# Gate and up products with the weight tiles stationary, and the down product between the two half units

## The reference

```python
D_MODEL = 1024
SEQ = 256
FFN_DIM = 2816            # D_FF = 2816 in the second block

def rmsnorm(x, g):
    xf = x.astype(jnp.float32)
    y = xf * lax.rsqrt(jnp.mean(xf * xf, axis=-1, keepdims=True) + RMS_EPS)
    return (y * g.astype(jnp.float32)).astype(x.dtype)

def swiglu(h, w_gate, w_up, w_down):
    return (jax.nn.silu(h @ w_gate) * (h @ w_up)) @ w_down

# first block
        ff = (jax.nn.silu(h @ w_ffn_gate[i]) * (h @ w_ffn_up[i])) @ w_ffn_down[i]
        x = x + rms_norm(ff, norm_ffn_post[i])
# second block, twice in each layer, with a residual weight of 0.5
        h = h + FFN_RESIDUAL_WEIGHT * swiglu(rmsnorm(h, ffn1_norm[layer]),
                                             ffn1_w_gate[layer], ffn1_w_up[layer], ffn1_w_down[layer])
```

## Time and profile before

| | |
|---|---|
| median of 3 runs | 1906.07 us (1905.44 to 1907.4) |
| span of the profiled execution, first to last instruction | 1904.2 us |
| PE busy | 1868.7 us, 98% of the span, 8988 matmuls |
| DVE busy | 1107.1 us, 58% |
| ACT busy | 958.9 us, 50% |
| POOL busy | 150.4 us, 8% |
| DMA | 332.72 MB, mean 175 GB/s |

### The profile page before, as it was taken

The page is one execution under the profiler, slowest core; times in us unless marked ns, Lnnn a source line. Parts: engine busy times, 40 slices in busy tenths (PEclk is TensorE's granted clock), DMA queues, the critical chain, the costliest instruction groups (busy, mean ns, idle before and its releaser), DMA issues.

```text
span 1904.2 us, 26150 instructions
## 1 busy us (share of the span) xinstructions
PE 1868.7 (98%) x8988; PEld 1523.3 (80%) x8988; DVE 1107.1 (58%) x1365; ACT 958.9 (50%) x1277; POOL 150.4 (8%) x259
## 2 busy tenths in 40 slices
PE   8999999999999999999999999999999999999998
PEld 7777888887877888888788887788888888868887
DVE  6666565448676575446754456655465445575454
ACT  5664454445675464445544446644454444564443
POOL 5210010001300010000100012000011000100000
PEclk9999999999999999999999999999999999999999
DMA  6335565554524546565655554455565564526553
GB/s 225 123 119 184 179 217 190 178 183 151 166 90 166 205 164 204 193 198 177 201 190 178 179 202 141 143 195 179 182 219 170 184 198 169 195 90 197 178 178 107
DMA packets 204987, 332.72 MB, mean 175 GB/s; under 512 B 11360, under 2 KB 150240, under 8 KB 204896
## 3 DMA queue, kind: packets, MB, share of 16 engines
q1 hardware_dynamic: 200240, 319.08, 49.9%
q0 software_dynamic: 3120, 11.02, 1.7%
q10 hardware_dynamic: 1536, 1.47, 0.2%
HBM read 330.48 MB, written 1.05 MB: 174 GB/s over the span
## 4 chain that ended last, share of the span: by engine, by line
PE 88%; issue 4%; DVE 3%; ACT 3%; DMA 1%; POOL 0%; DVEq 0%; SPq 0%; POOLq 0%; ACTq 0%
PE ps L571 27%; PE ps L565 27%; PE ps L556 27%; PE ps L598 3%; ACT whi L1254 1%; PE ps L771 1%; PE ps L759 1%; PE ps L787 1%; ACT prob L1352 1%; DVE wlo L1738 1%; DMA raw<-w_in_dram 0%; DVE prob L1878 0%; DMA xs<-x_dram 0%; DVE prob L1851 0%; DVE act_lo L1744 0%
## 5 line engine op out<-in xcount | busy, mean ns | idle before, releaser
L1738 DVE TENSOR_TENSOR wlo<-raw,whi 128x2048 fp32r<-128x2048 f32 (+1 forms) x306 | 690.6, 2257 | 510.3 <-ACT whi L1254 509.8
L1254 ACT ACTIVATE whi<-raw 128x2048 fp32r<-128x2048 f32 (+1 forms) x306 | 576.9, 1885 | 422.4 <-PE ps L565 422.3
L571 PE MATMUL ps<-whi,act_hi 128*128 128x512 f32 (+2 forms) x1632 | 442.0, 392 | 5.1 <-issue 2.4
L556 PE MATMUL ps<-wlo,act_hi 128*128 128x512 f32 (+2 forms) x1632 | 438.7, 387 | 0.0
L565 PE MATMUL ps<-whi,act_lo 128*128 128x512 f32 (+2 forms) x1632 | 432.2, 386 | 1.5 <-DVE act_lo L1744 1.5
L565 PEld LDWEIGHTS ps<-whi,act_lo 128*128 128x128 f32 x1632 | 303.9, 188 | 64.4 <-DVE act_lo L1744 2.3
L556 PEld LDWEIGHTS ps<-wlo,act_hi 128*128 128x128 f32 x1632 | 302.2, 188 | 61.8 <-issue 1.1
L571 PEld LDWEIGHTS ps<-whi,act_hi 128*128 128x128 f32 x1632 | 297.5, 188 | 64.1 <-issue 2.8
L1299 ACT ACTIVATE hid<-ps,stat 128x256 f32<-128x256 f32 x132 | 62.6, 474 | 282.9 <-PE ps L598 197.4
L2320 POOL TENSOR_TENSOR stat<-stat,eps 128x1 f32<-128x1 f32 x43 | 22.4, 521 | 1471.4 <-ACT prob L1286 1471.1
L1791 DVE SCALAR_TENSOR_TENSOR hid<-ps,stat,hid 128x256 f32<-128x256 f32 x132 | 63.6, 482 | 123.7 <-ACT hid L1299 123.7
(11 more groups left out here) (217 smaller groups left out, 1611.5 us busy)
## 6 DMA issues: line engine op xcount, KB each, us to landing
raw<-ffn_w_gate_dram SPq DMA_DIRECT2D x88, 512.0 KB, 4.0
raw<-ffn_w_up_dram SPq DMA_DIRECT2D x88, 512.0 KB, 5.0
raw<-ffn_w_down_dram SPq DMA_DIRECT2D x88, 512.0 KB, 3.9
raw<-w_in_dram SPq DMA_DIRECT2D x64, 512.0 KB, 4.4
raw<-w_ffn_gate_dram SPq DMA_DIRECT2D x44, 512.0 KB, 4.0
raw<-w_ffn_up_dram SPq DMA_DIRECT2D x44, 512.0 KB, 5.0
raw<-w_ffn_down_dram SPq DMA_DIRECT2D x44, 512.0 KB, 3.9
raw<-a_w_qkv_dram SPq DMA_DIRECT2D x24, 512.0 KB, 4.5
```

The lines of the kernel that those rows point to most:

```text
L556: last = nc.tensor.matmul(o, hi, a, start=False, stop=last_pass and stop and i == len(parts) - 1)
L571: nc.tensor.matmul(o, hi, a, start=start and i == 0, stop=False)
L1254: nc.scalar.activation(whi[:, u % SLOTS, 0:words], raw[:, u % SLOTS, 0:words], ACT.Copy)\
L1738: nc.vector.tensor_tensor(wlo[:, u % SLOTS, 0:words], raw[:, u % SLOTS, 0:words], whi[:, u % SLOTS, 0:words].bitcast(F32), ALU.subtract)\
```

## The change

Chunk 0 of a feed-forward part is computed as before. In chunks 1 to 10 gate and up take a 128x128 tile of weights as the stationary operand and the activations as the moving one (`columns`). The results come out turned, hidden features on the partitions and tokens along the columns, so nothing has to be transposed. `act_hi` and `act_lo` now lie side by side in one tile, and for each weight tile there are two matmuls: the hi weights against hi and lo activations at once (512 columns), and the lo weights against the hi activations (256 columns, added to the first half of the bank). A chunk's gate and up use four banks (0 to 3), and each unit is used in one go. The down product stands between the two units, and SP loads in that order.

The norm's factor is now along the columns. It is brought there once in each feed-forward part: DVE multiplies the identity by the factor (`spread_scale`), PE multiplies a tile of ones by that (`spread_scales`, two 128x128 matmuls), ACT copies the result. ACT copies the lo half of a bank to SBUF (`low_half`), DVE adds the hi half (`sum_parts`), DVE multiplies gate by the factor (`times_scale`), ACT takes silu, DVE multiplies by up, ACT rounds to `hid_hi`, DVE writes `hid_lo`. The up product's factor is left out and applied at the end of the feed-forward part, through the factor `fold` or `scale_of` in instructions that were there already. POOL has one memset more at the start.

```diff
                 gu(u, 0, 0)
                 gu(u + 1, 4, 0)
-                gu(u + 2, 0, CH)
-                gu(u + 3, 4, CH)
-                down(u + 4, 0)
-                with sp.Fori(0, NCH - 3) as i:
+                with sp.Fori(0, NCH - 2) as i:
                     w.chunk = i
-                    gu(u + 5, 0, i * CH + 2 * CH)
-                    gu(u + 6, 4, i * CH + 2 * CH)
-                    down(u + 7, i * CH + CH)
+                    gu(u + 2, 0, i * CH + CH)
+                    down(u + 3, i * CH)
+                    gu(u + 4, 4, i * CH + CH)
...
+                def spread_scales(tn):
+                    for t in range(T):
+                        free_before("turn", tn + t)
+                        pe.wait_ge(sem("spread"), w.at("spread", nth * T + t + 1))
+                        nc.tensor.matmul(ps[:, 2 + (tn + t) % 2, 0:P], ones[:, :], diagonal[:, t, :],
+                                         start=True, stop=True).then_inc(sem("turn_done"), 1)
...
+                def columns(u, half, gu, between=None, by_columns=False):
+                    unit_there(u)
+                    at = (slice(None), u % SLOTS, slice(None))
+                    vh, vl = (b[at].rearrange("p (k g n) -> p k g n", k=4, g=2) for b in (whi, wlo))
+                    order = [(g, j) for g in range(2) for j in range(CH // P)]
+                    if by_columns:
+                        order.sort(key=lambda at: at[1])
+                    for n, (g, j) in enumerate(order):
+                        if half == 0 and between is None and j == 0:
+                            free_before("gu", gu + g)
+                        elif half == 0 and g == 0 and between is not None:
+                            was_read("gu", gu - 2 + j)
+                        elif half == 0 and j == 0 and between is not None:
+                            between()
+                        bank = ps[:, 2 * g + j, :]
+                        cols = slice(j * P, (j + 1) * P)
+                        for k in range(4):
+                            kt = 4 * half + k
+                            nc.tensor.matmul(bank.rearrange("p (a n) -> p a n", a=2), vh[:, k, g, cols], both[:, :, kt, :],
+                                             start=half == 0 and k == 0, stop=False)
+                            last = nc.tensor.matmul(bank[:, 0:S], vl[:, k, g, cols], act_hi[:, kt, :],
+                                                    start=False, stop=half == 1 and k == 3)
+                        if half == 1 and n % 2 == 1:
+                            last.then_inc(sem("gu_done"), 1)
+                    if half == 0:
+                        last.then_inc(sem("used"), 1)
...
-                def chunk(u, gu, tn, start):
-                    tile = gate_up(u, gu)
-                    tile(0)
-                    turn_hidden(gu - T, tn)
-                    tile(1)
-                    down(u + 2, tn, start=start)
+                nth = gu // (2 * NCH)
+                _, diagonal, _ = scale_places(w)
                 tile = gate_up(u, gu, ready)
                 tile(0)
                 tile(1)
-                chunk(u + 2, gu + 2, tn, True)
+                def first_hidden():
+                    turn_hidden(gu, tn)
+                    spread_scales(tn + T)
+                    for t in range(T):
+                        was_read("turn", tn + T + t)
+                columns(u + 2, 0, gu + 2, first_hidden)
+                down(u + 3, 0)
+                columns(u + 4, 1, gu + 2)
                 with pe.Fori(0, NCH - 3) as i:
                     w.chunk = i
-                    chunk(u + 5, gu + 4, tn + 2, False)
+                    columns(u + 5, 0, gu + 4)
+                    down(u + 6, 1)
+                    columns(u + 7, 1, gu + 4)
                 w.chunk = None
-                u, gu, tn = u + UNITS_FFN - 4, gu + 2 * (NCH - 1), tn + 2 * (NCH - 1)
-                turn_hidden(gu - T, tn - T)
-                tile = gate_up(u, gu)
-                tile(0)
-                tile(1, (0,))
-                down(u + 2, tn - T, tiles=(0,))
-                turn_hidden(gu, tn, tiles=(0,))
-                tile(1, (1,))
-                down(u + 3, tn, tiles=(0,), stop=True)
-                turn_hidden(gu, tn, tiles=(1,))
-                down(u + 2, tn - T, tiles=(1,))
+                u, gu = u + UNITS_FFN - 4, gu + 2 * (NCH - 1)
+                columns(u, 0, gu)
+                columns(u + 1, 1, gu, by_columns=True)
+                down(u + 2, NCH - 2, tiles=(0,))
+                down(u + 3, NCH - 1, tiles=(0,), stop=True)
+                down(u + 2, NCH - 2, tiles=(1,))
                 if by_columns:
-                    down_by_columns(u + 3, tn)
+                    down_by_columns(u + 3, NCH - 1)
                 else:
-                    down(u + 3, tn, tiles=(1,), stop=True, between=between)
+                    down(u + 3, NCH - 1, tiles=(1,), stop=True, between=between)
...
+                for t in range(T):
+                    turned_hi(tn + t, hid_hi[:, :, t * P:(t + 1) * P], CH // P)
+                for t in range(T):
+                    turned_copy(tn + T + t, scale_row[:, t * P:(t + 1) * P].unsqueeze(1), 1)
+                with act.Fori(0, NCH - 2) as i:
                     w.chunk = i
-                    chunk(gu + 4, tn + 2)
+                    split(2)
+                    low_half(3, hid, 0)
+                    columns_silu(1)
+                    low_half(4, up_sum, 1)
+                    columns_hi(2)
+                    split(1)
                 w.chunk = None
-                done[0] += 3 * (NCH - 4)
-                last = NCH - 1
-                gu, tn = gu + 2 * last, tn + 2 * last
-                hidden_hi(tn - T)
-                silu(gu, 0, tn - T)
-                split(1)
-                hidden_hi(tn, (0,), tail[:, 0])
-                silu(gu, 1, tn - T)
-                split(1)
-                hidden_hi(tn, (1,), tail[:, 0])
+                done[0] += 3 * (NCH - 3)
+                split(1)
+                act.wait_ge(sem("hidden_lo"), w.at("hidden_lo", nth * NCH + NCH - 2))
+                for j in range(CH // P):
+                    js = slice(j, j + 1)
+                    low_half(2 * NCH - 1 + j, hid, 0, js)
+                    low_half(2 * NCH - 1 + j, up_sum, 1, js)
+                    columns_silu(2 * (NCH - 2) + 2 * j + 1, hid[:, j, :])
+                    columns_hi(2 * (NCH - 2) + 2 * j + 2, hid[:, j, :], tail[:, 0, j, :])
+                split(1)
...
+                def sum_parts(dst, g, js=slice(0, CH // P)):
+                    return nc.vector.tensor_tensor(dst, ps[:, 2 * g:2 * g + 2, 0:S][:, js, :], dst, ALU.add)
...
+                def columns(c):
+                    low_there(2 * c - 1)
+                    sum_parts(hid[:, :, :], 0).then_inc(sem("gu_read_v"), 1)
+                    was_summed(2 * c + 1)
+                    times_scale()
+                    low_there(2 * c)
+                    sum_parts(up_sum, 1).then_inc(sem("gu_read_v"), 1)
+                    was_summed(2 * c + 2)
+                    times_silu(T + c)
+                def hidden_lo(n, src=hid[:, :, :], lo=hid_lo[:, :, :], hi=hid_hi[:, :, :]):
+                    dve.wait_ge(sem("hidden_hi"), w.at("hidden_hi", nth * NCH + n))
+                    rest(lo, src, hi).then_inc(sem("hidden_lo"), 1)
+                def last_columns(c, j):
+                    js = slice(j, j + 1)
+                    low_there(2 * c - 1 + 2 * j)
+                    sum_parts(hid[:, js, :], 0, js).then_inc(sem("last_sum"), 1)
+                    low_there(2 * c + 2 * j)
+                    sum_parts(up_sum[:, js, :], 1, js).then_inc(sem("gu_read_v"), 1)
+                    dve.wait_ge(sem("last_sum"), w.at("last_sum", nth * (CH // P) + j + 1))
+                    times_scale(js)
+                    was_summed(2 * c + 1 + j)
+                    times_silu(T + c + j, js)
+                    hidden_lo(c + j, hid[:, j, :], tail[:, 1, j, :], tail[:, 0, j, :])
+                spread_scale(0)
+                times_up(0)
+                split(1)
+                spread_scale(1)
+                times_up(1)
+                split(1)
+                for t in range(T):
+                    at = (slice(None), slice(None), slice(t * P, (t + 1) * P))
+                    turned_lo(tn + t, hid_lo[at], hid_hi[at], CH // P)
+                _, name, k = w.read("turn", tn + 2 * T - 1)
+                dve.wait_ge(sem(name), w.at(name, k))
+                split(1)
+                with dve.Fori(0, NCH - 2) as i:
+                    w.chunk = i
                     split(1)
-                    times_up(gu, 1)
+                    columns(1)
+                    hidden_lo(1)
                     split(2)
-                inverse_there(norm)
-                times_up(gu, 0)
-                split(1)
-                inverse_there(norm + 1)
-                times_up(gu, 1)
-                split(1)
```

(15 more changed lines are left out.)

163 lines of the change are left out of this document (94 added, 69 removed).

## The result

The changed kernel takes 1948.56 us (median of 4 runs, 1946.35 to 1949.41), the kernel before, run alongside it, 1906.6 us. The ratio is 1.022, with a 95% interval from 1.0208 to 1.0232: 42 us slower. The direction was forecast, the size was not: +17.3 us was said, and 1948.56 lies above the upper end of the range, 1945.

The account below looks back on a forecast made before the run. PE's own pace was taken as the bound. -32.4 + 12.8 + 21.6 + 2.7 + 12.6 = +17.3 us took the span from 1904.2 to 1921.5, plus 1.9 for the median: 1923.4 us, range 1904 to 1945.

Parts of the forecast that it names:

- What bounds the kernel: Whole kernel: PE's own pace is the bound, busy 98% of the span, with the granted clock at its top.
- the steady state: Chunk loop: no wait added while 0.45 us of slack hold; a chunk takes 16.53 us against 16.81, gaining 0.28 us.
- Part 1: Feed-forward chunks: transposes removed, 5.4 us per feed-forward part, six times, -32.4 us.
- Part 2: Gate and up: 32 wide and 32 narrow matmuls instead of 48 wide, 0.21 us more per chunk, 60 chunks, +12.8 us.
- upper bound: Gate and up: an unhidden load bounds the narrow matmul at 0.188 us, 131 us more, 2054; a rival, chance 0.04.
- Part 3: Where chunk 1 begins: waits, turning and spreading cost 3.6 us, six times, +21.6 us; third feed-forward part +2.7 us, once.
- Part 4: Last chunk: PE waits for the hidden values 2.1 us, six times, +12.6 us.
- Rival 3: Chunk loop: PE waits at the gate banks if DVE is over 0.45 us later; 1940 to 1950, chance 0.19.
- Rival 1: Ends of each feed-forward part: half of the waits of Part 3 and Part 4 vanish; 1905, chance 0.12.
- 2's idea: Chunks 0 and 1: DVE isn't inside a split when PE asks, last chunk's halves overlap; -15 us, 1891, chance 0.08.

Follow-up runs that it names:

- The last experiment: The kernel with all three edits, with sixteen wide matmuls ahead of sixteen narrow ones in a chunk's second unit, instead of eight and eight: 1944.94 us, ratio 1.0198.
- the kernel with all three edits: Changed kernel with chunk 1's start and the last chunk rearranged, and eight wide matmuls ahead of eight narrow ones in the loop: 1904.89 us, ratio 0.9991.
- the grouped kernels: Changed kernel with four wide matmuls, then four narrow ones per bank: 1939.49 us; with groups of eight and both ends of a feed-forward part rearranged: 1904.89 us.
- The mended start: Changed kernel with turned values in banks 6 and 7, the factor spread behind the unit, DVE's rests ahead of its second split: 1925.43 us, ratio 1.0101.

## Why the prediction was wrong in size

- **What bounds the kernel** was right: PE's pace. So was the steady state: no wait, and the sum, `hidden_lo` and the splits came within 0.1 us of where they were placed. The last experiment shows what the order of the banks is worth: with 1.8 us less cover the loop waits.
- **Part 1, -32.4 us**: nothing shows it wrong. In the kernel with all three edits the loop's chunk is 16.61 us against 16.81, of the 0.28 forecast 0.20.
- **Part 2, +12.8 us: this step failed.** It took the price of a narrow matmul among narrow ones and that of a wide one among wide ones and added them. Each alone is right (0.1175 and 0.2267 measured), their alternation is not the sum: 0.353 us a pair instead of 0.347, and 0.06 us more in the down product behind. That is 0.27 us per chunk, 16 us in all: the term is +29 us where +12.8 was said, and the loop's whole gain of 0.28 us is gone. "The same columns" was counted, the 64 changes of width were not, and the "upper bound" of the step was a load's length, not the row that was missing from the trace: a wide one behind a narrow one. That the mix costs is shown by the grouped kernels; why it costs stays open.
- **Part 3**: first part 3.62 us against 3.6, third 3.1 us more than the first against 2.7. The mended start gave back 23.1 us; forecast was 24.3, less the 4.5 that turning and spreading cost without waits, 19.8; the rest is about the two clock drops fewer.
- **Part 4**: 1.58 and 1.88 us against 2.1; 10.7 us in sum against 12.6. The hand-overs were right in kind; the wait came out 0.2 to 0.5 us shorter.
- **The clock: a term that was left out.** The earlier trace rows had it at its top all along, and I carried it over to a kernel with new idle times of PE. It cost some 8 us in the profiled execution. Three of the five drops stood behind tail waits, and none was left there when these were filled.
- **The rivals**: none happened. Rival 3 has the right size for another reason, and the sixteen-wide kernel shows its mechanism when the gate banks come 1.8 us later. Rival 1's and 2's idea, that the ends could be kind, came true only once they were rewritten: from 1948.6 to 1914.7, without one change in the loop.

## What to carry to other kernels

Price a mix of operations by a row of the mix: where the trace has only rows of each kind alone, their sum can be too low, as here, and grouping the kinds is the first thing to try. Where a change adds idle time to a matmul engine at full clock, count also what the clock may take afterwards; a wait of 1.9 us cost 1.7 us more behind 10 of 20 such waits. Compare the clock of two profiles before a difference of a few microseconds is put down to the edit. And a producer's chain that never shows in a trace because it is hidden has to be measured before its start is moved: here it was 1.6 us long, and starting it 1.8 us later, 0.94 us before its result was wanted, cost as much as the whole change had.
